# A hybrid decoder block on one core: the front reordered by pairs of row tiles

## The chip, the core and the metric

The kernel runs on one core of one Trainium2 chip. The core has TensorE (PE: matmuls, and PEld for its weight loads), VectorE (DVE), ScalarE (ACT), GpSimd (POOL) and SyncE (SP, which here only issues DMAs), 16 DMA engines, an on-chip memory SBUF and a matmul result memory PSUM of eight banks. The metric is device microseconds for one launch. The kernel before takes 762.37 us, the median of three runs (762.04 to 762.8).

## The reference

One decoder block on x of 512 rows by 1024 columns, float32, in one layer:

```python
h = rmsnorm(x, g_mix)
proj = h @ w_in                       # 1024 -> q, k, v, u, gate_a, gate_s
q, k, v, u, gate_a, gate_s = jnp.split(proj, SPLITS, axis=-1)
attn = diff_attention(q, k, v, rel_bias, lam, subln_g, lam_init)
y = s5_ssm(u, ...)                    # u is 512 wide
z_val, z_gate = jnp.split(jax.nn.gelu(y) @ w_glu, 2, axis=-1)
mixed = sigmoid(gate_a) * attn + sigmoid(gate_s) * z_val * sigmoid(z_gate)
x = x + mixed @ w_out
h = rmsnorm(x, g_mlp)
x = x + jnp.square(jax.nn.relu(h @ w1)) @ w2
return rmsnorm(x, g_final)
```

`rel_bias` is a table of 32 buckets by 8 heads; the attention bias of a head is a row of 640 values (one for each distance) that is laid out along the diagonals.

## The kernel before

All large matmuls are float32 products made of three: a value is split into a high part (rounded to the fast matmul type) and a low part (the rest), and `mm3` issues high by high, high by low and low by high into the same PSUM bank. The weights come in **units** of 128 x 1024 values (512 KB). For each unit u, SP loads `raw[u % 4]`, ACT copies it to `w_hi` (`split_hi`, L636), and `w_lo = raw - w_hi` is made by POOL for units 0 to 3 (L561) and by DVE later (`split_lo`, L1032). The buffers form a ring of four. Each engine runs its own list of instructions in the order in which the code is written, and semaphores tie the lists together, so this order is what sets the schedule.

The front of the program has this work. Each **row tile** t (0 to 3) is 128 rows of x.

- SP (L392, L399) issues the four tiles of x into `mixA`, then `raw` of units 0 to 3, then the small constants, among them `rb` (the table `rel_bias`) and `oneh` (the one-hot matrix that spreads buckets to distances). ACT issues three small loads (`cols_nat`, L618), the norm gains.
- ACT squares and sums each tile of x (`V`, L621) and takes the root (`ms`, L624). DVE inverts it (`rstd`, L1011) and scales the tile (`mixA`, L1013).
- PE transposes the scaled tiles, 128 x 128 at a time, with `ident` as the other operand (L1722, 32 transposes): tile by tile, seven column blocks k of each, and block 7 last, since its bank holds the transposed gains first (L1734, copied to `cols` at L627). Each block k gets a bank of its own, filled by all four tiles.
- ACT copies the whole bank k (128 x 512) with the gain to `hT_hi` (`turn_hi`, L642), DVE makes `hT_lo` of it (`turn_lo`, L1004), eight blocks one after the other.
- PE then computes u in units 0 to 3 (the loop over `U_SSM` to `U_V`): unit u holds blocks 2u and 2u+1 of the weights; for each t, two blocks of three matmuls into bank 4 + t, so 24 matmuls of 128 x 512 a unit. Then come units 4 to 7 (half of v) and so on.

After unit 4, PE runs `turn_prm` (five small transposes of the parameters that DVE has computed in `prm`, L1762) and `bias_row` (L1769, L1770): the one-hot matrix by the table, 8 x 640, plain float32. DVE copies the result to `frow` (L1112, L1113), from where it goes to memory and returns as `bias` much later. The parameter chain on DVE (from L1046) starts when ACT has taken an exponential (L655), which stands in ACT's list after the copies of all eight blocks. Its instructions on `prm` are 16 x 128 values each.

Of the kernel before, what the change touches and what calls it, by code (L numbers as in the profile page):

```python
# [24 lines left out]
ACT = mybir.ActivationFunctionType  # L25
# [56 lines left out]
def build(nc, x, g_mix, w_in, lambda_q1, lambda_k1, lambda_q2, lambda_k2, subln_g, rel_bias,  # L82
# [132 lines left out]
    consts_in = sem("consts_in"); prm_in = sem("prm_in"); gfin_in = sem("gfin_in")  # L215
# [8 lines left out]
    scale_ready = sem("scale_ready"); x_rt = sem("x_rt"); x_rstd = sem("x_rstd"); x_scaled = sem("x_scaled")  # L224
    turned = sem("turned"); hT_hi_done = sem("hT_hi_done"); hT_lo_done = sem("hT_lo_done")
# [56 lines left out]

    NATS = 3 * 12
# [91 lines left out]
    def turn_bank(g, k):  # L375

        if g == 2 and k >= 4:
            return k - 4
        return (B_T + k) % 8 if g == 0 else B_T + k % 4
# [10 lines left out]
    def _(sp):  # L390
        for t in range(TOK):
            sp.dma_start(mixA[:, t, :], x[0, P * t:P * t + P, :]).then_inc(x_in[t], 16)  # L392
# [19 lines left out]
        for u in range(RING):  # L412
            load_raw(u)
# [5 lines left out]
        for src, dst in ((bass.AP(subln_g.tensor, 0, [[0, P], [1, V_DIM]]), gsub[:, :]),  # L419
# [4 lines left out]
                         (rel_bias, rb[:, :]), (onehot, oneh[:, :]),  # L424
# [108 lines left out]
    N_PRM, N_CONST, N_COLS = 3, 13, 3  # L533
# [15 lines left out]
    def _(pool):  # L549
# [59 lines left out]
    def _(act):  # L609
# [9 lines left out]
        for t in range(TOK):  # L619
# [4 lines left out]
            nc.scalar.activation(ms[:, 0, 1, t:t + 1], ms[:, 0, 0, t:t + 1], ACT.Sqrt, bias=eps_t[:, :],  # L624
                                 scale=1.0 / D_MODEL).then_inc(x_rt, 1)
        act.wait_ge(cols_turned, 1)
        nc.scalar.activation(cols[:, :], ps[:, turn_bank(0, KT - 1), 0:2 * KT + UT],  # L627
                             ACT.Identity).then_inc(cols_copied, 1)

# [354 lines left out]
    def _(dve):  # L984
# [24 lines left out]
        for t in range(TOK):  # L1009
# [629 lines left out]
    def _(pe):  # L1639
# [81 lines left out]
        def turn_x(t, k):  # L1721
            return nc.tensor.transpose(ps[:, turn_bank(0, k), P * t:P * t + P], mixA[:, t, P * k:P * k + P],  # L1722
                                       ident[:, :])

        pe.wait_ge(ident_set, 2)
        for t in range(TOK):
            pe.wait_ge(x_scaled, t + 1)
            for k in range(KT - 1):
                mm = turn_x(t, k)
                if t == TOK - 1:  # L1730
                    mm.then_inc(turned, 1)
            if t == 0:
                pe.wait_ge(cols_in, 16 * N_COLS)
                nc.tensor.transpose(ps[:, turn_bank(0, KT - 1), 0:2 * KT + UT], cols_nat[:, :],  # L1734
                                    ident[0:2 * KT + UT, 0:2 * KT + UT]).then_inc(cols_turned, 1)
        pe.wait_ge(cols_copied, 1)
        for t in range(TOK):
            mm = turn_x(t, KT - 1)
        mm.then_inc(turned, 1)


        for u in range(U_SSM, U_V):
            pe.wait_ge(w_lo_done, u + 1)
            for t in range(TOK):
                if u == U_SSM:
                    pe.wait_ge(hT_lo_done, t + 1)
                for k in (2 * u, 2 * u + 1):
                    if t == 0:
                        pe.wait_ge(hT_lo_done, k + 1)
# [16 lines left out]
        def bias_row():  # L1766
            pe.wait_ge(consts_in, 16 * N_CONST)
            pe.wait_ge(u_copied, 3)
            nc.tensor.matmul(ps[0:N_HEADS, 5, :], rb[:, :], oneh[:, 0:512], start=True, stop=True)  # L1769
            nc.tensor.matmul(ps[0:N_HEADS, 6, 0:BIAS_W - 512], rb[:, :], oneh[:, 512:BIAS_W], start=True,  # L1770
                             stop=True).then_inc(frow_mm, 1)

        def turn_c():
            for ri in range(2):
                if ri == 0:
                    pe.wait_ge(prm_copied, 1)
                else:
                    pe.wait_ge(frow_out, 2)
# [322 lines left out]
```

## Time and profile before

| | |
|---|---|
| median of three runs | 762.37 us |
| the profiled execution, whole | 762.46 us |
| its span, first to last instruction | 760.6 us |
| TensorE busy | 744.7 us, 98% of the span |
| VectorE, ScalarE, GpSimd busy | 65%, 47%, 7% |
| granted TensorE clock, mean | 0.999 |

A line of a timeline gives the start in us from the span's start, the duration, the engine, the line of the program, the operation, what it writes and reads, the shapes and how many it merges; in brackets, how long the engine sat idle before it and what ended that. A queue (SPq, ACTq) is the issuing of DMAs, not their transfer. A list of waits names who waited for whom and for how long in total. In the list by line and form, the last numbers are the total busy time and the mean duration of one in ns.

### The profile page before, as it was taken

Reading aid. Unit: us, or ns where it says so; the run is one execution under the profiler, and the core shown is the slowest. Engines: PE = TensorE matmul, PEld = TensorE weight load, DVE = VectorE, ACT = ScalarE, POOL = GpSimd, SP = SyncE. Lnnn points to the kernel's source line nnn. Section 1 sums busy time; section 2 is a strip of 40 time slices with the busy share of each in tenths; the row PEclk is TensorE's granted clock in tenths of the full one; section 3 lists DMA queues with packets and bytes.
Section 4 is the critical chain, followed back from the end, with each engine's and each line's share of the span. In section 5 each row is a group of like instructions: output and inputs, shape, how many; then the busy total and the mean of one; then the engine's idle time right before and its main releaser. Section 6 shows DMA issues by size and latency. Waiting matters only on the chain.

```text
span 760.6 us, 10038 instructions
## 1 busy us (share of the span) xinstructions
PE 744.7 (98%) x3754; PEld 609.2 (80%) x3754; DVE 498.1 (65%) x937; ACT 359.5 (47%) x630; POOL 54.0 (7%) x51
## 2 busy tenths in 40 slices
PE   5999999999999999999999999999999999999996
PEld 4878888777777777888888888888888888888884
DVE  4679999665556673436752667656676567646687
ACT  7524631265556663732421755434443345334454
POOL 3210000000000100000000110011000200020014
PEclk9999999999999999999999999999999999999999
DMA  7673339932223430236238563688177935796322
GB/s 249 197 163 119 100 109 165 202 104 72 70 69 119 159 111 2 84 110 249 84 111 236 124 167 83 166 244 198 56 166 234 229 91 110 196 247 145 83 50 111
DMA packets 99505, 106.19 MB, mean 140 GB/s; under 512 B 10540, under 2 KB 68576, under 8 KB 98432
## 3 DMA queue, kind: packets, MB, share of 16 engines
q1 hardware_dynamic: 93120, 87.05, 40.0%
q0 software_dynamic: 5504, 16.78, 12.1%
q10 hardware_dynamic: 832, 1.71, 1.1%
q8 instruction: 30, 0.49, 0.3%
q14 instruction: 19, 0.16, 0.1%
HBM read 89.70 MB, written 5.34 MB: 125 GB/s over the span
## 4 chain that ended last, share of the span: by engine, by line
PE 93%; DVE 3%; ACT 1%; issue 1%; DMA 1%; POOL 0%; SPq 0%; DVEq 0%; ACTq 0%
PE ps L1642 28%; PE ps L1644 28%; PE ps L1643 27%; PE ps L1932 3%; PE ps L1913 2%; PE ps L1922 1%; DMA mixA<-in_x 1%; PE ps L1717 1%; DVE w_lo L1435 1%; PE ps L1846 1%; ACT w_hi L636 1%; PE ps L1829 1%; DVE x L1484 1%; PE ps L1806 0%; PE ps L1850 0%
## 5 line engine op out<-in xcount | busy, mean ns | idle before, releaser
L1642 PE MATMUL ps<-hT_hi,w_hi 128*128 128x512 f32 x384 | 152.5, 397 | 0.3 <-DVE hT_lo L1004 0.3
L1644 PE MATMUL ps<-hT_hi,w_lo 128*128 128x512 f32 x384 | 149.9, 390 | 0.0
L1643 PE MATMUL ps<-hT_lo,w_hi 128*128 128x512 f32 x384 | 149.5, 389 | 0.0
L1642 PE MATMUL ps<-w_hi,hT_hi 128*128 128x512 f32 x288 | 113.9, 395 | 1.1 <-POOL w_lo L561 1.1
L1644 PE MATMUL ps<-w_hi,hT_lo 128*128 128x512 f32 x288 | 112.3, 390 | 0.0
L1643 PE MATMUL ps<-w_lo,hT_hi 128*128 128x512 f32 x288 | 112.1, 389 | 0.0
L1435 DVE TENSOR_TENSOR w_lo<-raw,w_hi 128x1024 fp32r<-128x1024 f32 x78 | 95.6, 1235 | 22.8 <-ACT w_hi L872 21.5
L872 ACT ACTIVATE w_hi<-raw 128x1024 fp32r<-128x1024 f32 x78 | 81.7, 1052 | 56.2 <-PE ps L1644 56.2
L636 ACT ACTIVATE w_hi<-raw 128x1024 fp32r<-128x1024 f32 x62 | 64.7, 1057 | 57.7 <-PE ps L1644 54.5
L1032 DVE TENSOR_TENSOR w_lo<-raw,w_hi 128x1024 fp32r<-128x1024 f32 x58 | 70.1, 1222 | 31.2 <-ACT w_hi L636 30.6
L1642 PE MATMUL ps<-w_hi,fa_hi 128*128 128x512 f32 x224 | 87.1, 389 | 0.0
L1643 PE MATMUL ps<-w_lo,fa_hi 128*128 128x512 f32 x224 | 87.1, 389 | 0.0
L1644 PE MATMUL ps<-w_hi,fa_lo 128*128 128x512 f32 x224 | 87.1, 389 | 0.0
L1642 PEld LDWEIGHTS ps<-hT_hi,w_hi 128*128 128x128 f32 x384 | 72.1, 188 | 16.0 <-DVE hT_lo L1004 0.5
L1644 PEld LDWEIGHTS ps<-hT_hi,w_lo 128*128 128x128 f32 x384 | 72.1, 188 | 15.4
L1643 PEld LDWEIGHTS ps<-hT_lo,w_hi 128*128 128x128 f32 x384 | 72.2, 188 | 14.1
L1642 PEld LDWEIGHTS ps<-w_hi,hT_hi 128*128 128x128 f32 x288 | 54.1, 188 | 13.0 <-POOL w_lo L561 1.3
L1644 PEld LDWEIGHTS ps<-w_hi,hT_lo 128*128 128x128 f32 x288 | 54.0, 188 | 11.4
L1643 PEld LDWEIGHTS ps<-w_lo,hT_hi 128*128 128x128 f32 x288 | 54.1, 188 | 10.7
L749 ACT ACTIVATE Pm<-Pm,nmx 128x128 f32<-128x128 f32 (+3 forms) x64 | 35.5, 556 | 31.6 <-DVE nmx L1325 30.9
L891 ACT ACTIVATE fs<-fr 128x512 f32<-128x512 f32 x32 | 20.2, 632 | 63.4 <-DVE fr L1448 63.2
L1320 DVE CUSTOM_DVE_ANT_0 Pm<-ps,bias 128x128 f32<-128x128 f32 (+3 forms) x64 | 28.9, 488 | 31.9 <-PE ps L1913 31.9
(258 smaller groups left out, 988.5 us busy)
## 6 DMA issues: line engine op xcount, KB each, us to landing
raw<-in_w SPq DMA_DIRECT2D x64, 512.0 KB, 4.9
raw<-in_w_in SPq DMA_DIRECT2D x44, 512.0 KB, 4.9
raw<-raw POOLq DMA_DIRECT2D x8, 1024.0 KB, 6.9
raw<-in_w_glu SPq DMA_DIRECT2D x8, 512.0 KB, 3.8
raw<-in_w_out SPq DMA_DIRECT2D x8, 512.0 KB, 3.7
T_w<-in_w SPq DMA_DIRECT2D x8, 512.0 KB, 6.7
T_w<-in_w POOLq DMA_DIRECT2D x8, 512.0 KB, 7.7
raw<-in_w POOLq DMA_DIRECT2D x8, 512.0 KB, 6.6
```

The lines of the kernel that those rows point to most:

```text
L636: nc.scalar.activation(w_hi[:, u % RING, :], raw[:, u % RING, :], ACT.Identity).then_inc(w_hi_done, 1)
L749: nc.scalar.activation(Pm[:, n % 2, m, 0:L], Pm[:, n % 2, m, 0:L], ACT.Exp, bias=nmx[:, n % 2, m:m + 1], accum_out=sums[:, n % 2, m:m + 1] ...
L872: nc.scalar.activation(w_hi[:, g % RING, :], src, ACT.Identity).then_inc(w_hi_done, 1)
L891: nc.scalar.activation(fs[:, q % 2, n % 2, :], fr[:, n % 2, :], ACT.Square).then_inc(f_sq, 1)
L1032: TT(w_lo[:, u % RING, :], raw[:, u % RING, :], w_hi[:, u % RING, :].bitcast(F32), ALU.subtract).then_inc(w_lo_done, 1)
L1320: nc.vector.tensor_tensor_reduce(out=Pm[:, n % 2, m, 0:L], in0=ps[:, score_bank(n, m), 0:L], in1=bias[:, h % 2, SEQ - L:SEQ], scale=1.0, s ...
L1435: TT(w_lo[:, g % RING, :], src, w_hi[:, g % RING, :].bitcast(F32), ALU.subtract).then_inc(w_lo_done, 1)
L1642: nc.tensor.matmul(dst, a_hi, b_hi, start=start, stop=False)
L1643: nc.tensor.matmul(dst, a_hi, b_lo, start=False, stop=False)
L1644: return nc.tensor.matmul(dst, a_lo, b_hi, start=False, stop=stop)
L1913: mm = nc.tensor.matmul(ps[:, score_bank(n, m), 0:L], qT[rows, h % 2, P * i:P * i + P], kT[rows, h % 2, 0:L], start=True, stop=True)
L1932: mm = nc.tensor.matmul(ps[:, B_O, P * i:P * i + P], wT[:, n % 2, P * j:P * j + P], V[:, j, V_DIM * h:V_DIM * h + V_DIM], start=(j == 0), ...
```

## The change

SP loads `rb` and `oneh` first, then tiles 0 and 1 of x, `raw` of unit 0, tiles 2 and 3, and the other three `raw`. The one-hot matmuls move from after unit 4 to the very start of PE's list, with their copies to `frow` between two scalings of DVE. After them PE issues six transposes of `ident` by itself, whose result nobody reads.

The transposed x is then built in pieces. For tiles 0 and 1 (a "pair"), blocks 0 to 3 are transposed first; ACT and DVE copy 128 x 256 pieces instead of 128 x 512. `w_lo` of unit 0 moves from POOL to DVE, in two halves around the first pair's low parts. PE starts unit 0 on tiles 0 and 1, transposes blocks 0 and 1 of tiles 2 and 3 in the middle of that unit, and the remaining blocks after unit 0 and inside unit 1. `x_place` lists which bank and columns each piece takes. ACT's list is reordered to match, with `split_hi(2)` and `split_hi(3)` ahead of copies that wait for PE's later transposes.

```diff
-        for t in range(TOK):
-            sp.dma_start(mixA[:, t, :], x[0, P * t:P * t + P, :]).then_inc(x_in[t], 16)
+        sp.dma_start(rb[:, :], rel_bias).then_inc(onehot_in, 16)
+        sp.dma_start(oneh[:, :], onehot).then_inc(onehot_in, 16)
+        load_x(0)
+        load_x(1)
+        load_raw(0)
+        load_x(2)
+        load_x(3)
+        for u in range(1, RING):
             load_raw(u)
@@ POOL
-        for u in range(U_V):
+        pool.wait_ge(w_lo_done, 1)
+        for u in range(1, U_V):
@@ ACT
+        hi_pair(0)
+        x_stats(2)
+        x_stats(3)
+        act.wait_ge(third_turned, 1)
+        for k in range(2):
+            x_hi(k, 2, 3, third_hi)
+        split_hi(1)
+        act.wait_ge(turned, 2)
+        for k in range(2):
+            x_hi(k, 3, 4, hT_hi_done)
+        hi_pair(1)
+        split_hi(2)
+        hi_late(1)
+        hi_pair(2)
+        hi_pair(3)
+        split_hi(3)
+        hi_late(2)
+        hi_late(3)
@@ DVE
+        scale_x(0)
+        scale_x(1)
+        dve.wait_ge(w_hi_done, 1)
+        dve.wait_ge(cols_copied, 1)
+        TT(w_lo[:, 0, 0:512], raw[:, 0, 0:512], w_hi[:, 0, 0:512].bitcast(F32), ALU.subtract).then_inc(w0_part, 1)
+        lo_pair(0)
+        TT(w_lo[:, 0, 512:], raw[:, 0, 512:], w_hi[:, 0, 512:].bitcast(F32), ALU.subtract).then_inc(w_lo_done, 1)
+        scale_x(2)
+        dve.wait_ge(frow_mm, 1)
+        TS(frow[:, 0:512], ps[0:N_HEADS, 7, :], 1.0, None, ALU.mult).then_inc(frow_out, 1)
...
+        scale_x(3)
@@ PE
+        pe.wait_ge(onehot_in, 32)
+        nc.tensor.matmul(ps[0:N_HEADS, 7, :], rb[:, :], oneh[:, 0:512], start=True, stop=True)
...
+        for _ in range(WARM):
+            nc.tensor.transpose(ps[:, 4, 0:P], ident[:, :], ident[:, :])
...
+                if u == U_SSM and t == 1:
+                    for t3 in range(2, TOK):
+                        pe.wait_ge(x_scaled, t3 + 1)
+                        for k3 in range(2):
+                            mm = turn_x(t3, k3)
...
+                if u == U_SSM + 1 and t == 1:
+                    turn_x_late(2)
+                if u == U_SSM + 1 and t == 2:
+                    turn_x_late(3)
+            if u == U_SSM:
+                turn_x_late(1)
+                turn_x_pair(2)
+                turn_x_pair(3)
...
             if u == U_V:
                 turn_prm()
-                bias_row()
```

PE's list at its start, before. All 32 transposes stand ahead of the first large matmul; "waits" names the semaphores.

```order
L1722 MATMUL ps<-ident,mixA 128x128 [waits x_scaled,ident_set]
L1722 MATMUL ps<-ident,mixA 128x128 x6
L1734 MATMUL ps<-ident,cols_nat 128x20 [waits cols_in]
L1722 MATMUL ps<-ident,mixA 128x128 [waits x_scaled]
L1722 MATMUL ps<-ident,mixA 128x128 x6
L1722 MATMUL ps<-ident,mixA 128x128 [waits x_scaled]
L1722 MATMUL ps<-ident,mixA 128x128 x6
L1722 MATMUL ps<-ident,mixA 128x128 [waits x_scaled]
L1722 MATMUL ps<-ident,mixA 128x128 x6
L1722 MATMUL ps<-ident,mixA 128x128 [waits cols_copied]
L1722 MATMUL ps<-ident,mixA 128x128 x3
L1642 MATMUL ps<-w_hi,hT_hi 128x512 [waits hT_lo_done,w_lo_done]
```

PE's list at its start in the changed kernel.

```order
L1828 MATMUL ps<-oneh,rb 8x512 [waits onehot_in]
L1829 MATMUL ps<-oneh,rb 8x128
L1833 MATMUL ps<-ident 128x128 [waits ident_set]
L1833 MATMUL ps<-ident 128x128 x5
L1835 MATMUL ps<-ident,cols_nat 128x20 [waits cols_in]
L1811 MATMUL ps<-ident,mixA 128x128 [waits x_scaled]
L1811 MATMUL ps<-ident,mixA 128x128 x3
L1811 MATMUL ps<-ident,mixA 128x128 [waits x_scaled]
L1811 MATMUL ps<-ident,mixA 128x128 x3
L1729 MATMUL ps<-w_hi,hT_hi 128x512 [waits pair_lo,w0_part]
```

The one-hot matmuls now come first, and only eight of the 32 transposes stand ahead of the first large matmul. The middle and the end of unit 0 on the same engine, changed kernel:

```order
L1811 MATMUL ps<-ident,mixA 128x128 [waits x_scaled]
L1811 MATMUL ps<-ident,mixA 128x128
L1811 MATMUL ps<-ident,mixA 128x128 [waits x_scaled]
L1811 MATMUL ps<-ident,mixA 128x128
L1729 MATMUL ps<-w_hi,hT_hi 128x512 [waits third_lo,frow_out]
...
L1729 MATMUL ps<-w_hi,hT_hi 128x512 [waits hT_lo_done]
...
L1811 MATMUL ps<-ident,mixA 128x128 x12
L1729 MATMUL ps<-w_hi,hT_hi 128x512 [waits pair_lo,w_lo_done]
```

Four transposes stand between tiles 1 and 2 of unit 0, twelve after it, and eight more inside unit 1 in two groups of four. VectorE's list at its start, before:

```order
L1011 RECIPROCAL rstd<-ms 128x1 [waits x_rt]
L1013 TENSOR_SCALAR mixA<-mixA,rstd 128x1024 [waits x_rstd]
L1004 SCALAR_TENSOR_TENSOR hT_lo<-ps,cols,hT_hi 128x512 [waits hT_hi_done,cols_copied]
L1004 SCALAR_TENSOR_TENSOR hT_lo<-ps,cols,hT_hi 128x512 [waits hT_hi_done] x7
L1046 TENSOR_TENSOR prm<-prm,dtt 16x128 [waits prep_act]
```

The first two rows there are the last of four scalings. In the changed kernel, after two scalings:

```order
L1089 TENSOR_TENSOR w_lo<-raw,w_hi 128x512 [waits cols_copied,w_hi_done]
L1072 SCALAR_TENSOR_TENSOR hT_lo<-ps,cols,hT_hi 128x256 [waits pair_hi]
L1072 SCALAR_TENSOR_TENSOR hT_lo<-ps,cols,hT_hi 128x256
L1091 TENSOR_TENSOR w_lo<-raw,w_hi 128x512
L1065 RECIPROCAL rstd<-ms 128x1 [waits x_rt]
L1067 TENSOR_SCALAR mixA<-mixA,rstd 128x1024 [waits x_rstd]
L1094 TENSOR_SCALAR frow<-ps 8x512 [waits frow_mm]
L1095 TENSOR_SCALAR frow<-ps 8x128
L1065 RECIPROCAL rstd<-ms 128x1 [waits x_rt]
L1067 TENSOR_SCALAR mixA<-mixA,rstd 128x1024 [waits x_rstd]
L1072 SCALAR_TENSOR_TENSOR hT_lo<-ps,cols,hT_hi 128x128 [waits third_hi]
L1072 SCALAR_TENSOR_TENSOR hT_lo<-ps,cols,hT_hi 128x128
```

The last two scalings now stand behind the first pair's low parts, both halves of `w_lo` and, for tile 3, the two copies to `frow`.

## Rows read from the trace of the kernel before

**Rows 1.** The page: busy time of TensorE and others, chain that ended last
```profile
PE 744.7 (98%) x3754; PEld 609.2 (80%) x3754; DVE 498.1 (65%) x937; ACT 359.5 (47%) x630; POOL 54.0 (7%) x51
PE 93%; DVE 3%; ACT 1%; issue 1%; DMA 1%; POOL 0%; SPq 0%; DVEq 0%; ACTq 0%
```
**Rows 2.** Waits of TensorE, 0 to 70 us: total, times, longest
```profile
PE ps L1722 <- DVE mixA L1013: 6.8, 2, 6.6
PE ps L1642 <- POOL w_lo L561: 1.1, 1, 1.1
```
**Rows 3.** Timeline of 0 to 15 us, all engines, in parts
```profile
0.74 1.83 SPq L392 DMA_DIRECT2D mixA<-in_x  x4
...
3.98 1.06 ACT L621 ACTIVATE V<-mixA 128x1024 f32<-128x1024 f32 x1 [1.75 <-DMA mixA<-in_x]
...
5.36 1.04 ACT L621 ACTIVATE V<-mixA 128x1024 f32<-128x1024 f32 x1
...
5.68 0.75 DVE L1013 TENSOR_SCALAR mixA<-mixA,rstd 128x1024 f32<-128x1024 f32 x1
...
7.88 1.06 ACT L621 ACTIVATE V<-mixA 128x1024 f32<-128x1024 f32 x1 [1.06 <-DMA mixA<-in_x]
...
9.42 0.49 SPq L431 DMA_DIRECT2D rb<-in_rel_bias  x1
...
10.70 1.05 ACT L636 ACTIVATE w_hi<-raw 128x1024 fp32r<-128x1024 f32 x1
...
11.83 2.36 POOL L561 TENSOR_TENSOR w_lo<-raw,w_hi 128x1024 fp32r<-128x1024 f32 x1 [10.26 <-ACT w_hi L636]
12.19 1.84 ACT L642 ACTIVATE hT_hi<-ps,cols 128x512 fp32r<-128x512 f32 x3 [0.45 <-PE ps L1722]
...
14.24 0.50 PE L1642 MATMUL ps<-w_hi,hT_hi 128*128 128x512 f32 x1 [1.06 <-POOL w_lo L561]
```
**Rows 4.** The transposes of x on TensorE in the same timeline
```profile
6.58 1.73 PE L1722 MATMUL ps<-ident,mixA 128*128 128x128 f32 x7 [6.58 <-DVE mixA L1013]
...
10.40 2.79 PE L1722 MATMUL ps<-ident,mixA 128*128 128x128 f32 x18 [0.18 <-DVE mixA L1013]
...
11.76 1.18 PEld L1722 LDWEIGHTS ps<-ident,mixA 128*128 128x128 f32 x11 [0.31 <-DVE mixA L1013]
```
**Rows 5.** Loads of the four tiles of x (L392), issue to landing
```profile
DMA to landing us min/median/max: 3.2/5.1/7.0
```
**Rows 6.** Groups by line and form: pieces of the sizes that the change uses
```profile
L758 ACT ACTIVATE wT<-ps 128x256 f32<-128x256 f32 x8 | 3.0, 379 | 0.1
L1458 DVE TENSOR_TENSOR fa_lo<-fs,fa_hi 128x512 fp32r<-128x512 f32 x16 | 11.1, 693 | 4.2 <-ACT fa_hi L901 4.2
L1320 DVE CUSTOM_DVE_ANT_0 Pm<-ps,bias 128x256 f32<-128x256 f32 x16 | 6.2, 422 | 0.0
L1320 DVE CUSTOM_DVE_ANT_0 Pm<-ps,bias 128x128 f32<-128x128 f32 x16 | 4.0, 289 | 22.7 <-PE ps L1913 22.6
```
**Rows 7.** Timeline of TensorE around the one-hot matmuls, 41 to 44 us
```profile
41.14 0.39 PE L1643 MATMUL ps<-w_lo,hT_hi 128*128 128x512 f32 x1
41.37 0.39 PE L1644 MATMUL ps<-w_hi,hT_lo 128*128 128x512 f32 x1
...
42.10 1.02 PE L1769 MATMUL ps<-oneh,rb 32*8 32x512 f32 x2
...
43.27 0.50 PE L1642 MATMUL ps<-w_hi,hT_hi 128*128 128x512 f32 x1
```
**Rows 8.** Timeline of VectorE, 20 to 43 us, in parts
```profile
20.37 1.06 DVE L1046 TENSOR_TENSOR prm<-prm,dtt 16x128 f32<-16x128 f32 x1 [1.39 <-ACT dtt L655]
...
21.36 0.27 DVE L1047 TENSOR_TENSOR prm<-prm,dtt 16x128 f32<-16x128 f32 x1
...
24.70 2.32 DVE L1074 TENSOR_SCALAR prm<-prm 16x128 f32<-16x128 f32 x1
...
42.20 0.24 DVE L1107 COPY mag<-ps 128x80 f32<-128x80 f32 x1 [7.92 <-PE ps L1762]
```

More of the change, by code:

```diff
@@ L378, in turn_bank, with x_place, x_turned @@
             return k - 4
-        return (B_T + k) % 8 if g == 0 else B_T + k % 4
+        return B_T + k % 4
+    def x_place(t, k):
+        c0 = 256 * (k % 2) + P * (t % 2)
+        bank = (2 if t == 2 else 3) if t >= 2 and k < 2 else ((0, 1, 2, 3), (None, 0, 1, 0))[t // 2][k // 2]
+        return bank, c0
+    def x_turned(k, t0, t1):
+        bank, c0 = x_place(t0, k)
+        return ps[:, bank, c0:c0 + P * (t1 - t0)]
     def wait_rows(eng, c, t):
@@ L618, in _, with x_stats @@
             act.dma_start(dst, src).then_inc(cols_in, 16)
-        for t in range(TOK):
+        def x_stats(t):
             act.wait_ge(x_in[t], 16)
@@ L1006, in turn_lo, with scale_x @@
             ins.then_inc(hT_lo_done, 1)
-        for t in range(TOK):
+        def scale_x(t):
             dve.wait_ge(x_rt, t + 1)
@@ L1683, in nat_free @@
             if c == 0:
+                pe.wait_ge(pair_lo, KT)
                 pe.wait_ge(hT_lo_done, KT)
@@ L1736, in _, with turn_x_pair, turn_x_late @@
[L1736 to L1739, printed above, removed]
+            bank, c0 = x_place(t, k)
+            return nc.tensor.transpose(ps[:, bank, c0:c0 + P], mixA[:, t, P * k:P * k + P], ident[:, :])
+        def turn_x_pair(g):
+            for t in range(2):
+                for k in (2 * g, 2 * g + 1):
+                    mm = turn_x(t, k)
+            mm.then_inc(pair_turned, 1)
+        def turn_x_late(g):
+            for t in range(2, TOK):
+                for k in (2 * g, 2 * g + 1):
+                    mm = turn_x(t, k)
+            mm.then_inc(turned, 2)
@@ new lines, in _ @@
+        pe.wait_ge(onehot_in, 32)
+        nc.tensor.matmul(ps[0:N_HEADS, 7, :], rb[:, :], oneh[:, 0:512], start=True, stop=True)
+        nc.tensor.matmul(ps[0:N_HEADS, 6, 0:BIAS_W - 512], rb[:, :], oneh[:, 512:BIAS_W], start=True,
+                         stop=True).then_inc(frow_mm, 1)
+        pe.wait_ge(ident_set, 2)
+        for _ in range(WARM):
+            nc.tensor.transpose(ps[:, 4, 0:P], ident[:, :], ident[:, :])
+        pe.wait_ge(cols_in, 16 * N_COLS)
+        nc.tensor.transpose(ps[:, 5, 0:2 * KT + UT], cols_nat[:, :],
+                            ident[0:2 * KT + UT, 0:2 * KT + UT]).then_inc(cols_turned, 1)
@@ new lines, in _, with first_waits @@
+        pe.wait_ge(x_scaled, 1)
+        for k in range(4):
+            turn_x(0, k)
+        pe.wait_ge(x_scaled, 2)
+        for k in range(4):
+            mm = turn_x(1, k)
+            if k % 2:
+                mm.then_inc(pair_turned, 1)
+        def first_waits(t):
+            if t == 0:
+                pe.wait_ge(w0_part, 1)
+                pe.wait_ge(pair_lo, 1)
+            elif t == 1:
+                pe.wait_ge(cols_copied, 1)
+            elif t == 2:
+                pe.wait_ge(frow_out, 2)
+                pe.wait_ge(third_lo, 2)
+            else:
+                pe.wait_ge(hT_lo_done, 2)
@@ L1764, in turn_prm @@
             mm.then_inc(prm_turned, 1)
[L1766 to L1771, printed above, removed]
         def turn_c():
```

95 lines of the change are left out of this document (62 added, 33 removed).

## The prediction

> **What bounds the kernel now.** I read the page first: TensorE is busy for 744.7 us, and 93% of the chain that ended last is TensorE [rows 1]. Then its waits in the first 70 us: 6.8 us for the first scaled tiles and 1.1 us for the low part of unit 0, and no other [rows 2]. From the first large matmul at 14.24 on [rows 3] TensorE is never out of work in that stretch, so the front matters only through two numbers: when the large matmuls start, and how much else is put between them afterwards. The sum is made on the profiled execution (762.46 us whole, 760.6 of span), 0.1 us from the median of 762.37; a difference found on it is added to the median.
>
> The timeline of the front [rows 3] shows the chain to 14.24. Tile 0 of x lands at 3.98; its scaling starts 1.70 later (5.68) and takes 0.75. Tile 2 lands at 7.88, although tile 1 was there before 5.36. The high part of unit 0 runs from 10.70 for 1.05, POOL makes the low part from 11.83 for 2.36, and TensorE starts 0.05 later. All 32 transposes lie ahead of that, in time in which TensorE waits anyway: the first seven at 0.213 apart or 1.73 in all, the last eleven 0.109 apart, 1.18 in all [rows 4].
>
> **Part 1, the loads.** SP issues `rb` (0.49) and `oneh` ahead of x; a tile's issue takes 0.46 (four in 1.83), and `oneh` is taken at that [rows 3]. So each x load starts 0.9 later: tile 0 lands at 4.9 instead of 3.98. The four tiles took 3.2 to 7.0 from issue to landing with a median of 5.1 [rows 5]. With issues at 0.74, 1.2, 1.65 and 2.1, and tile 2 at 7.88 (6.2 from issue), the fourth number is 4.0: tile 1 landed at 5.2 and tile 3 at 9.1. Tiles thus land 1.3 apart except between 1 and 2, where it was 2.65, a stall of 1.35. If the stall belongs to its time (5.2 to 6.5), it now hits tile 1, which would land at 7.4; if it belongs to the third transfer, tile 1 lands at 6.1. I take 7.0, nearer the late end, since ScalarE's small loads beside it keep their time. `raw` 0 is now the third transfer in place of the fifth: 7.88 + 0.9 = 8.8 in both cases.
>
> **Part 2, the start of unit 0.** Tile 1 at 7.0: scaling from 8.7 to 9.5 (1.70 and 0.75). The second block's transpose ends its way to ScalarE about 0.55 later, 10.1 (0.43 for one, by 11.76 to 12.19 [rows 3, 4], and 0.11 for the next). The high part of unit 0 is done at 9.85 (8.8 + 1.05), its first low half on VectorE by 10.55 (0.69 [rows 6]). Two high pieces of 128 x 256 at 0.38 each end at 10.85, the first low piece at 0.42 [rows 6] at 11.3. **The first large matmul starts at 11.35, 2.9 earlier than 14.24.** With tile 1 at 6.1 it is 11.15, since then `raw` 0 sets the chain; at 7.4 it is 11.8.
>
> **Part 3, new waits inside unit 0.** The three matmuls of the first block end at 12.15. VectorE finishes the second low piece at 11.7 and the second half of `w_lo` at 12.35 (0.69): a wait of 0.2. Tiles 0 and 1 are done at about 14.6. Tile 2's statistics start on ScalarE only after the first pair, at 10.85, and tile 3's 1.38 behind (5.36 less 3.98 [rows 3]); VectorE scales tile 2 from 12.4, copies `frow` (two copies, 0.8), and scales tile 3 until 15.1. The third tile's low pieces (2 x 0.29 [rows 6]) follow at about 15.65 to 16.3, and tile 2's matmuls start at 16.35. That is 1.75 after 14.6, of which 0.44 are four transposes: a wait of 1.3. Tile 3 waits 0.1 for its two pieces behind `split_hi(1)`. Together **+1.6**, and each restart costs 0.1 more than a matmul in the stream: **+0.3**. A later tile 1 moves all of this along unchanged.
>
> **Part 4, transposes among the matmuls.** 24 of the 32 now stand behind the first large matmul, at 0.109 [rows 4]: **+2.6**, with 0.25 for four changes between the two kinds (a matmul after a group takes about 0.1 more to come). In the old order they cost nothing. They replace no wait: those after unit 0 come when `w_lo` of unit 1 is nearly ready anyway (its high part ends at 16.8, POOL's 2.36 at 19.2), and TensorE arrives at 19.4.
>
> **Part 5, the one-hot matmuls.** They lay on TensorE's stream from 42.10 to 43.27: **-1.17** [rows 7]. At the front they run at half the rate, 2.2 us, from about 3.5 when `oneh` (80 KB) has landed; six transposes of `ident` add 1.3, which ends at 7.0. The first transposes of x are wanted at 7.4 and 9.5. If `oneh` lands 1 us later, it still hides.
>
> **Part 6, the parameter chain.** The exponential that starts it stands behind all copies, the last of which needs transposes inside unit 1: unit 1 from 20.8, its first three tiles with two groups of transposes 5.0, the way to ScalarE 0.45, two pieces 0.75 and the exponential with its table 1.5 (estimated from the 1.39 that VectorE waited for it). The chain starts at about 28.4 instead of 20.37 [rows 8], 8 later. It had 7.92 of idle time at its end, before 42.20, and TensorE's call moves 1.9 later with the stream (0.7 and the 1.17 that only go after it). Two of its instructions took 1.06 and 2.32 beside POOL's `w_lo`, where the next of the same shape took 0.27 [rows 8]; in the new order POOL has finished by 25.5, which gives 2.8 back. So it ends some 4 us before it is needed: **0**. Should it be late, `turn_prm` and with it every later matmul would wait. The Trainium skill has this as its rule of the shared port pair (SBUF - State Buffer, "SBUF: two separate sides"): a GpSimd instruction and a VectorE instruction with two SBUF inputs lock each other out. An instruction in a two-port mode falls under it too. By that rule VectorE's new halves of `w_lo` meet no GpSimd work, and the sum stays.
>
> **Sum.** -2.9 + 1.6 + 0.3 + 2.6 + 0.25 - 1.17 = +0.7. So **763.1 us**: the front starts 2.9 earlier and pays it back in transposes and waits that lay in idle time before.
>
> **Rivals.**
> - *Stall on tile 1 in full.* Tile 1 at 7.4 adds 0.45: 763.5. For it speaks that the stall has a time at which other transfers run; against it nothing but one trace.
> - *No stall near the front, faster.* Tile 1 at 6.1 and, because the stall falls behind `raw` 0, that at 7.5: then the pair's transposes set the chain, at 10.65 for the first matmul. 0.7 less, and if the pieces overlap more than their durations say (three of ScalarE's 128 x 512 took 1.84 [rows 3], and each of VectorE's may hide 0.1 of the one ahead), VectorE's list is up to 1 us shorter by the third tile: 761.7 down to 760.4. To be faster by over 0.2% the waits of Part 3 would have to vanish too, since -2.9 + 2.85 - 1.17 is only -1.2.
> - *The clock, slower.* TensorE now has eight transposes up to about 9.9 and then nothing until 11.35. In the trace the transposes went at 0.213 until 10.9 and at 0.109 after it, 4.4 us after the first [rows 4]; after the wait of 1.06 before 14.24 the matmuls came at the full rate. If the longer hole, behind a thinner start, leaves the array at the lower rate, the first 12 to 15 matmuls take 0.45 in place of 0.23 (41.14 to 41.37 [rows 7]); that is some 3 us, of which the waits of Part 3 absorb 1.3: +1.7, 764.8. It decides from the moment the rate is still low at the first large matmul. The Trainium skill (TensorE: Matmul & The Clock Gate, Part 1) says that the array runs at half its clock when idle and at the full one after sustained work; the six transposes of `ident` serve that rule, the hole works against it. The granted clock of this case's page shows only 0.999 over the span, so no row settles it.
> - *The order does not fit its own transfers, slower.* Tile 3's scaling stands behind `frow` and tile 2's statistics behind the pair. If ScalarE's pieces of 256 come at 0.45 rather than 0.38 and each handover costs 0.1 more, the three rounds between ScalarE and VectorE in unit 0 add 0.8: 763.9 to 764.3.
> - *The parameter chain is late.* More than 3 us would have to be missing in Part 6; then 764 and above.
>
> **How the numbers follow.** Forecast with its neighbour, tile 1 between 6.5 and 7.4 (762.8 to 763.6): 0.45. No stall, 760.4 to 762.5: 0.22. Clock: 0.12. Slow handovers: 0.14. Parameter chain and the like: 0.03. A gain further back in the program that no row here shows, below 760.85: 0.04. Two executions of one kernel lie within 0.4 us here, and about 0.2%, 1.5 us, is what a measurement can tell from no change. So "same" reaches from 760.85 to 763.9. Faster: 0.04 and a third of the case without a stall, 0.11. Slower: clock, parameter chain, half of the handovers and 0.05 for the forecast's upper edge together with them, 0.27. Same: 0.62. The range is 761.3 to 764.9.
>
> **What would show it.** In the profile of the changed kernel: the first large matmul at 11.2 to 11.8; tile 1's square starting at 6.3 to 7.4; a wait of TensorE of about 1.3 us between tiles 1 and 2 of unit 0, released by `hT_lo` of VectorE; unit 1 starting at 20.6 to 21.2 (before: 19.8, by 14.24 and 24 matmuls at 0.23); no one-hot matmul near 42, and the same matmul of unit 5 that started at 43.27 within 1.2 us of that. The forecast is wrong if the first matmul comes before 10.5, if matmuls of unit 0 are 0.4 apart (clock), or if TensorE waits for `prm` near 42.

## The result: 11 us slower, and the profile after

| | before | changed |
|---|---|---|
| median (six runs each, beside one another) | 762.48 us | 773.79 us |
| lowest and highest | 762.04, 762.85 | 772.56, 774.93 |
| the profiled execution, whole; its span | 762.46; 760.6 | 774.75; 772.9 |
| granted TensorE clock, mean | 0.999 | 0.993 |

The ratio is 1.0146, with a 95% interval of 1.0136 to 1.0157. The forecast was 763.1, the range 761.3 to 764.9: the time lies 9 us beyond its upper end. The waits of TensorE in the first 80 us of the changed kernel (what waited, for whom, total, times, longest) have a line that the kernel before lacks altogether [rows 2]:

```profile
PE ps L1927 <- POOL u_pairs L590: 6.3, 1, 6.3
PE ps L1729 <- DVE hT_lo L1072: 3.3, 2, 2.0
PE ps L1828 <- DMA oneh<-in_onehot: 3.2, 1, 3.2
PE ps L1811 <- DVE mixA L1067: 0.6, 2, 0.3
```

The first line is 64 us into the program, at a step (`turn_u`) that the change does not touch. There u, which the front has computed, comes back from memory, GpSimd copies it into pairs (`u_pairs`), and TensorE transposes it 16 times.

**The front.** The timeline of TensorE from 8 us on, changed kernel:

```profile
8.94 1.12 PE L1811 MATMUL ps<-ident,mixA 128*128 128x128 f32 x4 [0.25 <-DVE mixA L1067]
12.10 0.77 PE L1729 MATMUL ps<-w_hi,hT_hi 128*128 128x512 f32 x1 [2.04 <-DVE hT_lo L1072]
12.66 0.63 PE L1730 MATMUL ps<-w_lo,hT_hi 128*128 128x512 f32 x1
13.09 0.63 PE L1731 MATMUL ps<-w_hi,hT_lo 128*128 128x512 f32 x1
...
17.36 0.62 PE L1811 MATMUL ps<-ident,mixA 128*128 128x128 f32 x4
19.20 0.47 PE L1729 MATMUL ps<-w_hi,hT_hi 128*128 128x512 f32 x1 [1.23 <-DVE hT_lo L1072]
19.51 0.39 PE L1730 MATMUL ps<-w_lo,hT_hi 128*128 128x512 f32 x1
19.74 0.40 PE L1731 MATMUL ps<-w_hi,hT_lo 128*128 128x512 f32 x1
...
23.30 0.48 PE L1729 MATMUL ps<-w_hi,hT_hi 128*128 128x512 f32 x1
...
46.64 0.50 PE L1729 MATMUL ps<-w_hi,hT_hi 128*128 128x512 f32 x1
```

Read the starts, not the durations. The first large matmul comes at 12.10, 2.1 earlier than before [rows 3]. But it and the eleven behind it are 0.43 apart (12.66 to 13.09); behind the four transposes at 17.36 they are 0.23 apart (19.51 to 19.74). Before, all were 0.23 apart. The granted clock reads 1.00 in these stretches all the same; that this is TensorE's lower rate is read from the spacing, which is the same 0.43 behind the wait at 70 us, at a granted 0.50. Twelve matmuls at 0.2 more are 2.4 us. The wait of 1.23 ahead of tile 2 is the one that Part 3 put at 1.3. Unit 1 starts at 23.30, and unit 5's first matmul at 46.64, where it stood at 43.27 [rows 7]: **the front costs 3.4 us**, not 0.7.

**The turn of u.** The chain that ended last, 40 to 75 us, in order of time (start, duration, what), the middle of it:

```profile
41.52 6.71 DMA u_dram<-u_sb
...
48.26 0.64 SPq L458
...
48.94 18.61 DMA u_nat<-u_dram
...
67.60 2.86 POOL u_pairs L590
...
70.51 3.67 PE ps L1927 x16
```

u's store to memory starts at 41.52, its load at 48.26, and the second half of the load takes 18.61 us. Two more rows, of ScalarE's and of SP's queue, stand beside it:

```profile
46.42 0.79 ACTq L765 DMA_DIRECT2D frow_dram<-frow  x1
48.26 5.41 SPq L458 DMA_DIRECT2D u_nat<-u_dram  x2
```

The store of `frow` to memory (L765: eight rows of 640 values, each written 32 times, 640 KB) now starts 1.84 us *ahead* of u's load. These are the same DMAs in the kernel before, from the timelines of the two queues:

```profile
36.98 0.41 ACTq L674 DMA_DIRECT2D u_dram<-u_sb  x1
...
44.35 0.79 ACTq L711 DMA_DIRECT2D frow_dram<-frow  x1
```
```profile
41.38 1.30 SPq L438 DMA_DIRECT2D u_nat<-u_dram  x2
```

Here the load had a lead of 2.97 us, and its halves landed 5.0 and 6.6 us after issue. Now both have moved, but unequally. The `frow` store moved by 2.07, since it no longer waits for one-hot matmuls behind unit 4. The load moved by 6.88: 4.54 because unit 3 ends later (3.37 at unit 5, and the 1.17 of one-hot matmuls that only go after it), and 2.3 because u's store took 6.7 instead of 4.4 us. Beside that store now runs the load of unit 9's weights, `raw` 9, which before had been issued 2.7 us ahead of it. It waits for a `w_lo` of VectorE that stands inside the parameter chain. Before, then changed:

```profile
33.06 1.23 DVE L1032 TENSOR_TENSOR w_lo<-raw,w_hi 128x1024 fp32r<-128x1024 f32 x1
34.32 0.37 SPq L399 DMA_DIRECT2D raw<-in_w_in  x1
```
```profile
40.02 1.23 DVE L1124 TENSOR_TENSOR w_lo<-raw,w_hi 128x1024 fp32r<-128x1024 f32 x1
41.27 0.37 SPq L413 DMA_DIRECT2D raw<-in_w_in  x1
```

So the later parameter chain (31.01 in place of 20.37) reaches the turn of u by this way.

What the wait costs is more than its 6.3 us. The 16 transposes took 1.91 before and now 3.67, +1.8, and some three matmuls behind them are 0.43 apart, +0.6. The table by stretch has the reason (per row: from:to, length, busy PE, PEld, DVE, ACT, POOL, granted clock, DMA share, GB/s):

```profile
60.00:65.00 5.00, 4.19 (x19) 3.14 (x17) 5.00 (x3) 2.39 (x4) 0.00 (x0) 1.00 1.00 187
65.00:70.00 5.00, 0.00 (x0) 0.00 (x0) 4.96 (x4) 1.06 (x1) 2.40 (x1) 0.86 1.02 260
70.00:75.00 5.00, 4.49 (x19) 4.30 (x20) 4.88 (x7) 2.57 (x5) 0.46 (x1) 0.50 0.21 81
```

While TensorE waited, the granted clock fell to 0.50, the lower of its two levels (1.2 GHz). Together **8.7 us for the turn of u**; with the front's 3.4 that is 12.1 of the 12.3 us between the two spans. The medians lie 11.3 apart. The profiled execution is 1.0 above its median, and its front is the slowest of five profiles of this front: unit 5's first matmul comes at 46.64 here and at 45.55, 45.56, 45.60 and 46.59 in four of the experiments, so the front costs 2.3 to 3.4 us.

### The profile page after: what moved, and what is told of

Same layout as the page of the kernel before. It is cut to its first block, busy times and chain, and to the rows that moved or that the text cites. A ratio compares the mean times of both kernels' runs of the same rounds, so it can differ in the third digit from the quotient of the medians.

```text
span 772.9 us, 10074 instructions
## 1 busy us (share of the span) xinstructions
PE 751.6 (97%) x3760; PEld 613.2 (79%) x3760; DVE 498.1 (64%) x949; ACT 361.7 (47%) x640; POOL 52.5 (7%) x50
## 4 chain that ended last, share of the span: by engine, by line
PE 89%; DMA 4%; DVE 3%; issue 1%; ACT 1%; POOL 0%; SPq 0%; DVEq 0%; ACTq 0%
PE ps L1729 26%; PE ps L1731 26%; PE ps L1730 26%; PE ps L2064 3%; PE ps L2045 2%; DMA u_nat<-u_dram 2%; PE ps L2054 1%; DMA raw<-in_w_in 1%; DMA u_dram<-u_sb 1%; PE ps L1805 1%; DVE w_lo L1522 1%; PE ps L1979 1%; PE ps L1962 1%; DVE x L1571 0%; PE ps L1927 0%
## 5 line engine op out<-in xcount | busy, mean ns | idle before, releaser
L1729 PE MATMUL ps<-w_hi,hT_hi 128*128 128x512 f32 x288 | 115.6, 401 | 3.3 <-DVE hT_lo L1072 3.3
L1731 PEld LDWEIGHTS ps<-hT_hi,w_lo 128*128 128x128 f32 x384 | 72.1, 188 | 15.3
```

What stands on the lines that cost most here:

```text
L1729: nc.tensor.matmul(dst, a_hi, b_hi, start=start, stop=False)
L1731: return nc.tensor.matmul(dst, a_lo, b_hi, start=False, stop=stop)
```

## The experiments

Ten kernels. The first theory was that two separate faults make up the loss, the low rate in the front and, at the turn of u, a load slowed by the `frow` store; its rival, that the load is late by itself or that something else holds GpSimd's copy. "u + 5" in the diffs is the place in SP's list behind unit 9's `raw`.

### Who delays the turn of u

**The `frow` store behind the copy of u's transposes**, issued at 73.2 in place of 46.42; nothing else is changed.

```diff
@@ ACT, earlier in the list
-                act.wait_ge(frow_out, 2)
-                act.dma_start(frow_dram, frow[:, :].unsqueeze(1).to_broadcast(...)).then_inc(frow_done, 16)
@@ ACT
                 copy_ut()
+                act.wait_ge(frow_out, 2)
+                act.dma_start(frow_dram, frow[:, :].unsqueeze(1).to_broadcast(...)).then_inc(frow_done, 16)
```

> The changed kernel with one move: ScalarE issues the store of frow (640 KB) after it has copied the turned u, that is after u_nat has landed, instead of before copy_c. Theory C (collision): the 6.3 us wait of TensorE for u_pairs in the changed kernel comes from the store of frow, issued 1.8 us ahead of the load of u_nat and slow (about 50 KB a us for 11 us). Then u_nat lands within 7 us, TensorE does not wait there and stays at its full rate: 773.8 - 6.3 - 2.0 (sixteen transposes and the first matmuls at half rate behind the wait) = 765.0 to 766.0. Rival L (late chain): the load of u_nat is late because the store of u and raw 9 are late; then at least 4 us of the wait stay: 769 or more.

Measured: 773.55 us (772.63 to 774.74), ratio 1.0147 [1.0132, 1.0162]. **Not a microsecond came back**, a plain miss. Yet the load did what it should: its halves landed 5.1 and 6.7 us after issue. The time is the rival's (769 or more), and half of its reason holds: the load was late, not for TensorE, which came to the turn at 63.1, but for VectorE. The timelines of GpSimd and of VectorE in this kernel show what took the transfer's place:

```profile
54.56 14.88 POOL L590 COPY u_pairs<-u_nat 128x2048 f32<-128x2048 f32 x1 [3.47 <-DMA u_nat<-u_dram]
```
```profile
54.31 2.29 DVE L1254 TENSOR_TENSOR BL<-Bb,turned_powers 128x2048 f32<-128x2048 f32 x1
56.52 2.29 DVE L1255 TENSOR_TENSOR bl_t<-Bb,turned_powers 128x2048 f32<-128x2048 f32 x1
58.72 1.23 DVE L1124 TENSOR_TENSOR w_lo<-raw,w_hi 128x1024 fp32r<-128x1024 f32 x1
...
65.39 2.29 DVE L1261 TENSOR_TENSOR bl_t<-Bb,turned_powers 128x2048 f32<-128x2048 f32 x1
67.72 3.86 DVE L1263 TENSOR_TENSOR BL<-BL,bl_t 128x2048 f32<-128x2048 f32 x1
```

GpSimd's copy, 1.89 us long in the kernel before, took 14.88. It arrived 0.25 us after VectorE had begun a row of eight TENSOR_TENSORs, each with two inputs in SBUF, that follow one another without a pause. The first gap in that row is before L1263, which waits for the result of L1261 (67.68 to 67.72). The copy ended at 69.44, 1.76 behind it, and L1263 itself took 1.6 longer than its like. So, by these times, the copy did its work from 67.7 on and waited 13 us for its turn.

That is the shared port pair of Part 6 again, which was weighed there only for `w_lo`. The Trainium skill (SBUF - State Buffer, "SBUF: two separate sides") says that whichever of the two instructions starts first gets the pair for its whole duration and the other blocks. This trace agrees as to the lock, but it was not handed over at the end of the instruction in whose way the copy stood. It stayed with VectorE over seven of them.

**VectorE made to wait for the copy.** To tell the port from other causes, one line is added to the kernel above: VectorE starts its row only when the copy is done.

```diff
         dve.wait_ge(turned, KT)
+        dve.wait_ge(u_paired, 1)
         settle()
```

> e1 (store of frow later, raw 9 left where it is) with one wait more: VectorE begins its row of long two-input instructions only when GpSimd's copy u_pairs is done. Theory P: the load lands at about 54.6 as in e1, the copy takes about 1.9 us in place of 14.9, VectorE starts its row at 56.5 instead of 54.3, TensorE does not wait at turn_u: 765 to 766.5. Rival (the load's landing is what TensorE waits for, whatever VectorE does): 772 or more, as e1.

Measured: 766.89 us (a single time), 6.7 less for one wait, and 0.4 above the expected range; its front was 1.0 slower than that of the kernel without the wait (46.59 against 45.60 at unit 5). Timelines of GpSimd and VectorE:

```profile
55.70 1.90 POOL L590 COPY u_pairs<-u_nat 128x2048 f32<-128x2048 f32 x1 [3.63 <-DMA u_nat<-u_dram]
```
```profile
57.80 2.29 DVE L1255 TENSOR_TENSOR BL<-Bb,turned_powers 128x2048 f32<-128x2048 f32 x1 [2.41 <-POOL u_pairs L590]
```

The copy takes 1.90 again, and TensorE no longer waits at the turn. VectorE's row starts 2.4 later. TensorE does not miss it in the next 50 us. Later it waits 0.2 for `taps` and, near 153 us, 0.5 for a `w_lo`, both of VectorE and neither found in the kernel before; no run shows whether they come from the later row. The kernel before has the other order, the copy first and then a small VectorE instruction with two SBUF inputs, whose like took 0.18:

```profile
49.28 1.89 POOL L569 COPY u_pairs<-u_nat 128x2048 f32<-128x2048 f32 x1
49.34 1.88 DVE L1143 TENSOR_TENSOR powers<-pwt 128x32 f32<-128x32 f32 x1
```

It ended at 51.22, 0.05 behind the copy. The exclusion between the two engines is thereby shown; that it is the port pair is the Trainium skill's reading of it.

**u's load one place earlier in SP's list**, ahead of `raw` 9, the `frow` store left where the change has it.

```diff
-            if u == U_V + 5:
+            if u == U_V + 4:
                 load_u()
```

> The changed kernel with SyncE's load of u_nat put ahead of raw 9 instead of behind it, so that the 512 KB of raw 9 no longer compete with the store of u. Theory C: the store of u lands about 2 us sooner (near 46 instead of 48.2), u_nat is issued about when the store of frow is, and shares the DMA engines with it: still slow, 3 to 6 us of waiting stay: 770 to 774. Theory L: the wait goes: 766 or less, if raw 9 is not late itself.

Measured: 769.04 us (a single time), 1 below the 770 to 774 that were expected of the collision. u's store now took 4.5 us instead of 6.7, so `raw` 9 right ahead of it had cost it 2.2. The load was issued at 44.97, with a lead of 0.37 over the `frow` store at 45.34, and this is the list of its transfers (issue to landing), and GpSimd's copy:

```profile
DMA to landing us min/median/max: 4.9/11.7/18.4
```
```profile
64.12 1.93 POOL L590 COPY u_pairs<-u_nat 128x2048 f32<-128x2048 f32 x1 [13.08 <-DMA u_nat<-u_dram]
```

The second half took 18.4 us: the `frow` store alone slows it (the next kernel, where only that store stands later, has 6.6). The copy ran at once, by luck: VectorE had nothing to do from 64.30 to 66.27, since it waited for a high part of ScalarE's. TensorE waited 3.0. So there are two ways to a wait there, and either is enough: a late load, or a load that lands when VectorE's row has begun.

**Both moves.** The `frow` store behind the copies and the load ahead of `raw` 9:

> The changed kernel with both moves of the last two runs: the store of frow behind the copies of the turned u, and the load of u_nat ahead of raw 9. Theory P (port): in e1 the load landed at 54.6, 0.2 us after VectorE's row of six long two-input instructions had begun (54.3), and GpSimd's copy u_pairs then took 14.9 us instead of 1.9, until VectorE's first pause; with both moves u_nat lands near 50.5, the copy takes about 2 us ahead of that row, TensorE does not wait at turn_u and stays at its full rate: 764.8 to 765.8. Rival: the copy is slow for another reason (the load, or GpSimd itself): 769 or more.

Measured: 765.2 us (764.31 to 766.09), ratio 1.0027 [1.001, 1.0045]; the kernel before beside it had 762.98. GpSimd, and VectorE's last instructions ahead of its row:

```profile
52.27 1.90 POOL L590 COPY u_pairs<-u_nat 128x2048 f32<-128x2048 f32 x1 [1.23 <-DMA u_nat<-u_dram]
```
```profile
52.44 2.36 DVE L1243 COPY turned_powers<-powers 128x32 f32<-128x32 f32 x8
54.72 1.21 DVE L1124 TENSOR_TENSOR w_lo<-raw,w_hi 128x1024 fp32r<-128x1024 f32 x1
55.85 2.28 DVE L1254 TENSOR_TENSOR BL<-Bb,turned_powers 128x2048 f32<-128x2048 f32 x1
```

The copy comes first now, and it is VectorE that is held up: the eight small copies took 2.36 in place of 0.78, off the path. TensorE has no wait at the turn. Of the loss of 11.3 us 2.2 are left, as expected, and they are the front's: unit 5 starts at 45.56, 2.3 later than before. (Between the two profiled executions it is 10.1 us that went, 1.4 more than the turn's 8.7; nine matmuls were at 0.43 in this profile, not twelve, which is 0.6 of it.)

**The same collision in the kernel before.** If the theory holds, the old front must fail as well once its lead is gone. In the kernel before, the one-hot matmuls move behind unit 2 and their copies ahead in VectorE's list; nothing of the front is changed. (The waits that guard their PSUM banks move with them and are left out here.)

```diff
-                bias_row()
@@ in the loop over the units
+            if u == U_SSM + 2:
+                pe.wait_ge(consts_in, 16 * N_CONST)
+                pe.wait_ge(hT_lo_done, KT)
+                nc.tensor.matmul(ps[0:N_HEADS, 0, :], rb[:, :], oneh[:, 0:512], start=True, stop=True)
+                nc.tensor.matmul(ps[0:N_HEADS, 1, 0:BIAS_W - 512], rb[:, :], oneh[:, 512:BIAS_W], start=True,
+                                 stop=True).then_inc(frow_mm, 1)
```

> The kernel before with the one-hot matmuls after unit 2 instead of after unit 4, and their copies ahead of the copy of the turned parameters, so that the store of frow is issued at about 41.9 instead of 44.35. The front, raw 9 and the store of u are as before. Theory C with the order deciding: u_nat is issued at 41.4, half a us ahead of the store of frow, and most of its packets are queued first: some slower than before (6 to 10 us to land), no wait of TensorE: 762 to 763. If any overlap is enough: u_nat takes 15 us or more and TensorE waits 2 to 6 us: 765 to 769.

Measured: 770.23 us (a single time), 7.8 more than the kernel before beside it (762.39), and above both expected ranges. The load was issued at 42.77 (1.39 later) and the `frow` store at 43.28 (1.07 sooner): a lead of 0.5 instead of 2.97. The load's second half took 16.2 us, then the copy met VectorE's row, and TensorE the copy:

```profile
59.74 7.60 POOL L569 COPY u_pairs<-u_nat 128x2048 f32<-128x2048 f32 x1 [10.75 <-DMA u_nat<-u_dram]
...
67.39 3.58 PE L1794 MATMUL ps<-ident,u_pairs 128*128 128x128 f32 x16 [6.35 <-POOL u_pairs L569]
```

An edit that takes work from nobody and moves two small matmuls loses 7.8 us, most of the turn's 8.7. The load thus needs a lead of somewhere between 0.5 and 3.0 us. The kernel before has 3.0, so at most 2.5 of it was to spare, and nothing in its waits shows it. Moving the one-hot matmuls, a part of the change that was priced at -1.17, is by itself a way to lose 8.

### What the front costs

**Filling the hole with transposes.** In the kernel with the later `frow` store, eleven transposes of `ident` follow the first pair's.

```diff
+    FILL = 11
...
+        for _ in range(FILL):
+            nc.tensor.transpose(ps[:, 4, 0:P], ident[:, :], ident[:, :])
```

> e1 with eleven more transposes of ident on TensorE behind the first pair's eight transposes, in the hole of 2.4 us ahead of the first large matmul. Theory H (the hole keeps the array at half rate): the rate rises before or soon after the first large matmul at 12.1; eleven of the twelve first matmuls 0.2 shorter, 2.2 us less up to the wait between tiles 1 and 2, of which about 0.6 stays as a longer wait for the third pieces: 1.5 to 2.2 us below e1. Rival R (the rise has a time of its own, or transposes of ident do not bring it): no difference to e1, within 0.4.

Measured: 772.47 us (772.08 to 772.92), ratio 1.0134 [1.0117, 1.0151]: 1.1 less than the same kernel without them, where 1.5 to 2.2 were expected. The mechanism is there, and at unit 5's first matmul so is its size (43.78 against 45.60, 1.8); 0.7 of it does not arrive at the end, and no run shows where it goes. The transposes themselves go from 0.21 to 0.11 apart at 11.3, the large matmuls start at 11.71, and all of them are 0.23 apart. The turn of u still has its 6.4: VectorE's row starts 1.8 sooner too (52.50), the load lands at 54.34, and the copy takes 13.27.

**Both moves and the fill:**

> e4 with the eleven transposes of ident in the hole ahead of the first large matmul. Theory P and theory H together: 1.1 to 1.6 below e4 (the clock's part), 763.4 to 764.4, which is where the sum of the prediction (763.1) had put the changed kernel without its two faults. If the sum of the front was wrong beside the two faults: 765 or more, or below 762.5.

Measured: 763.71 us (763.47 to 765.43), ratio 1.0015 [1.0006, 1.0025], 1.5 less than without the fill. The profiled execution is one of the longer ones, 764.79 whole (TensorE waits 1.0 for a `w_lo` of VectorE between 145 and 160 us), but its front can be read:

```profile
10.69 1.46 PE L1847 MATMUL ps<-ident 128*128 128x128 f32 x8
11.90 0.48 PE L1730 MATMUL ps<-w_hi,hT_hi 128*128 128x512 f32 x1
12.22 0.39 PE L1731 MATMUL ps<-w_lo,hT_hi 128*128 128x512 f32 x1
...
16.57 0.47 PE L1730 MATMUL ps<-w_hi,hT_hi 128*128 128x512 f32 x1 [1.24 <-DVE hT_lo L1073]
...
43.99 0.50 PE L1730 MATMUL ps<-w_hi,hT_hi 128*128 128x512 f32 x1
```

Unit 5 starts at 43.99, 0.72 later than before. **That is the +0.7 of the prediction's sum**, and it is what the change's front costs when both faults are out of it.

**Without the six transposes at the start** (`WARM = 0`, on the kernel with both moves):

> The kernel with both moves at the turn of u and the front of the change, with the six transposes of ident at the start left out (WARM = 0). In the kernel with them 9 large matmuls ran 0.427 apart and the time was 765.2. If the six do nothing for the clock, the rate rises where it rose there (about 15.5 to 16) and the time stays within 0.5 us, 764.7 to 765.7. Rival: they bring the rise forward, and without them some 5 to 8 more large matmuls run at 0.427: 766.2 to 766.8.

Measured: 764.51 us (763.83 to 765.48), ratio 1.0028 [1.0016, 1.004], against 1.0027 with them (0.7 us below that kernel's median and just below the expected range, but the kernel before beside it was 0.7 lower too, 762.26 against 762.98). The first large matmul came at 11.37 and the matmuls went to 0.23 apart at 14.44, no later than with the six (15.3). So the change's warm-up does nothing that can be measured.

**Tile 2's transposes one tile earlier.** On the kernel with both moves and the fill, tile 2 is transposed between tiles 0 and 1, and the `frow` copies stand ahead of `w_lo`'s first half on VectorE.

```diff
-                if u == U_SSM and t == 1:
-                    for t3 in range(2, TOK):
+                if u == U_SSM and t < 2:
+                    for t3 in range(t + 2, t + 3):
```

> e6 with tile 2's two transposes one tile earlier (after tile 0 of unit 0, tile 3's stay after tile 1) and the copies to frow on VectorE ahead of the first half of w_lo. The wait of 1.24 us ahead of tile 2's matmuls is a round trip from TensorE over ScalarE and VectorE that starts only after tile 1; started one tile earlier it should nearly vanish: 0.9 to 1.2 below e6, 762.3 to 763.4. Rival: the scaling of tile 2 is what comes last, and TensorE then waits for it after tile 0 (under 0.4 gained).

Measured: 762.86 us (761.77 to 763.98), ratio 1.0002 [0.9992, 1.0011]. The wait ahead of tile 2 is gone (the first large matmul 12.43, unit 5 at 43.77, though the same eleven transposes brought the full rate only at about 13.4 in this profile), and the change with its repairs stands level with the kernel before.

**x ahead of the one-hot table**, with the one-hot matmuls and three transposes in the hole, and twelve transposes at the start:

> The kernel with both moves at the turn of u, and a front in another order: SP issues x tiles 0 and 1 and raw 0 first and rb and oneh behind them; TensorE runs 12 transposes of ident at the start, and the two one-hot matmuls and 3 transposes of ident between the first pair's transposes and the first large matmul; tile 2's transposes stand one tile earlier. If what holds the front is the 0.9 us of issue ahead of x, tile 0's square starts at 4.1 to 4.5, raw 0 has landed before 8.3, the first large matmul starts at 11.0 to 11.5 at the full rate of 0.23, and the time is 761.6 to 762.6. Rival: the landing of raw 0 does not follow its place in the queue (between profiles of one order it moved between 8.0 and 9.7), and the time stays at 762.6 to 763.4. Second rival: the frow copies now come late on VectorE and give the wait before tile 2 back, 1.2 us: 763.5 and more.

Measured: 763.85 us (762.82 to 767.27), ratio 1.0022 [1.0011, 1.0033]; 761.6 to 762.6 was expected. ScalarE's start on tile 0 and on `raw` 0, and TensorE, in its timeline:

```profile
4.10 1.06 ACT L644 ACTIVATE V<-mixA 128x1024 f32<-128x1024 f32 x1 [1.87 <-DMA mixA<-in_x]
...
8.71 1.06 ACT L661 ACTIVATE w_hi<-raw 128x1024 fp32r<-128x1024 f32 x1 [1.09 <-DMA raw<-in_w_in]
...
9.22 1.87 PE L1843 MATMUL ps<-oneh,rb 32*8 32x512 f32 x2
...
12.57 0.63 PE L1731 MATMUL ps<-w_lo,hT_hi 128*128 128x512 f32 x1
13.00 0.63 PE L1732 MATMUL ps<-w_hi,hT_lo 128*128 128x512 f32 x1
```

Tile 0 came 0.96 sooner than in the changed kernel, as its place in the queue says. `raw` 0 did not: it was usable at 8.71, no better than in the other profiles (7.91 to 9.65, with two issues ahead of it), which is the first rival named there. And although TensorE paused nowhere from 7.10 on, its matmuls stayed 0.43 apart until 16.4. Neither the expectation nor its rivals had said that; the wait ahead of tile 2, which the second rival expected, did not come. The eleven transposes had brought the full rate at 11.3 in two profiles and at 13.4 in a third; this filler, in its one profile, did not bring it before the time at which it came without any filler.

## Why the prediction was wrong

- **A DMA and a meeting place had no term.** This is the step that failed, in Parts 5 and 6 of the sum, and it is worth 8.7 of the 10.7 us by which the forecast was short. Part 5 counted what the one-hot matmuls take from TensorE. It did not follow their result: `frow` comes free earlier, and ScalarE's store of 640 KB with it. It also did not ask what unit 3's later end moves: u's store, the load behind it, GpSimd's copy. The prediction knew that TensorE's stream there would be 1.9 later (the sum's 0.7 and the 1.17), but used this for the parameter chain only. And Part 6 held the end of that chain against TensorE's call alone. The low part inside it, for which `raw` 9 waits, ended 7.0 later (41.25 against 34.29) and put that load beside u's store: 2.3 of the 6.9 us by which u's load moved. The DMAs could have been found by asking, of each issue between 33 and 50 us, what releases it and what runs beside it.
- **The exclusion of GpSimd and VectorE was asked about at one place only.** Part 6 used it in favour of the change, where VectorE's halves of `w_lo` met no GpSimd work. The one long GpSimd copy of this stretch, 3.1 us ahead of VectorE's long row in the kernel before (49.28 + 1.89 against 54.24), was not looked for.
- **The clock rival was true, by the spacing of the matmuls.** It had a chance of 0.12 and a price of +1.7. The twelve matmuls at 0.43 were forecast (12 to 15), the place was right, and so was the test ("0.4 apart"). But its price was cut by 1.3 for waits that it would absorb, and they stayed: the wait ahead of tile 2 was 1.23 with and 1.24 without the slow matmuls. Tile 2's matmuls started 1.84 and 1.83 us behind tile 2's transposes (17.36 to 19.20, 14.74 to 16.57), and these stand behind the slow matmuls on TensorE: the wait moves along with them. VectorE's list, in which Part 3 saw the cause, was idle for 3.0 and 1.0 us there. By unit 5's start (45.56 without the fill, 43.99 with it) the rate cost 1.6 in the kernel with both moves and 2.4 by count in the changed kernel.
- **The start.** Tile 0 came at 5.06 (4.9 forecast), tile 1 at 6.44: no stall (7.0). `raw` 0 at 9.65, where 8.8 was said, held the first large matmul at 12.10 instead of 11.35. In the experiments with the same list of loads ScalarE began on it between 7.9 and 9.4, so this term has an error of its own of nearly 1 us.
- **The parts that held.** The wait ahead of tile 2, 1.24 for 1.3. Waits, restarts and transposes together: from 11.90 to 43.99 in the kernel with both moves and the fill is 32.09; before, 14.24 to 43.27 less 1.17 is 27.86; so 4.2 where 1.6 + 0.3 + 2.85 = 4.75 stood. Start half a microsecond late, the rest half a microsecond less: +0.72 for +0.7, and that the two cancel is luck. The parameter chain started at 31.01 (28.4 forecast) and ended in time for TensorE's call; its cost came by way of `raw` 9, as said above.

## What to carry to other kernels

When an edit shifts the time at which a stage ends, list every DMA within some 10 us of that point, on all queues, with what releases each, and see which of them keep their distance: here one moved by 2.1 and another by 6.9, and a lead of 3 us that no wait shows was the whole margin. Do the same for a GpSimd instruction and the next unbroken row on VectorE; if one must come first, say so with a wait, which here gave 6.7 us and cost at most 0.7 us that can be seen. A moved instruction is priced by what its result sets free, not only by its own time.

## What the runs showed of the hardware

- **GpSimd can be locked out for a whole row of VectorE instructions.** A copy of 1.9 us took 14.9, 13.3, 7.6 and 2.9 us in four kernels, by when it arrived. In all four it ended 1.75 us after L1261's end (L1262 in the kernel with the fill, L1174 in the kernel before with the store moved), the first instruction of the row whose successor has to wait for its result: 69.44 less 67.68, 67.61 less 65.86, 67.34 less 65.59, 70.45 less 68.70.
- **One store can slow another queue's load nearly threefold.** The same load of two halves took 5.0 and 6.6 us with the store of 640 KB issued 3.0 us behind it, and 4.8 and 16.2, 4.9 and 18.4, 9.7 and 18.6 with the store 0.5 and 0.4 us behind and 1.8 us ahead. What in the store does it (its size, or its pieces of 640 values) is not shown.
- **The profile's granted clock did not show the slow start.** It reads 1.00 in the stretches from 7 to 22 us, where matmuls of 512 columns were 0.427 apart, as they are behind the wait at 70 us at a granted 0.50. The distance between starts is the better witness there.
- **What raised the rate** is open beyond these rows. Without a filler it rose between 14.4 and 17.8 us in six profiles, five of which have the same front, so its time varies by over 2 us by itself. With eleven 128 x 128 transposes in the hole it rose at 11.3, 11.3 and 13.4. With two one-hot matmuls and three transposes there it rose at 16.4 in one profile, no sooner than without. Six transposes at the start made no difference.
